# Last attention layer: softmax sink sums and gated splits moved to GpSimd, output panels 0 and 1 split and partly multiplied between the units

## The reference

```
m    = max(sink, max_j s_j)
den  = exp(sink - m) + sum_j exp(s_j - m)
p_j  = exp(s_j - m) / den
o    = sum_j p_j v_j
x   += g * ((o * silu(z)) @ w_out)        # w_out: 1024 x 1024
```

## Time and profile before

| | us |
|---|---|
| median of 3 runs | 1967.74 (1966.52 to 1968.47) |
| the profiled execution, whole | 1967.9 |
| its span, first to last instruction | 1965.7 |
| PE busy | 1928.1 (98% of the span) |
| DVE busy | 1303.1 (66%) |
| ACT busy | 905.4 (46%) |
| GpSimd busy | 52.1 (3%) |

### The profile page before, as it was taken

The page is one execution under the profiler, slowest core; times in us unless marked ns, Lnnn a source line. Parts: engine busy times, 40 slices in busy tenths (PEclk is TensorE's granted clock), DMA queues, the critical chain, the costliest instruction groups (busy, mean ns, idle before and its releaser), DMA issues. The chain is left out here.

```text
span 1965.7 us, 31270 instructions
## 1 busy us (share of the span) xinstructions
PE 1928.1 (98%) x12652; PEld 1619.4 (82%) x12652; DVE 1303.1 (66%) x2407; ACT 905.4 (46%) x1635; POOL 52.1 (3%) x78
## 2 busy tenths in 40 slices
PE   7999999999999999999999999999999999999998
PEld 5788668889888888898689899998887788888867
DVE  5547777857886665667666777675566464555886
ACT  4446863325423232355764655443443432234685
POOL 0000000001000000000000000000000000001000
PEclk9999999999999999999999999999999999999999
DMA  7322016543545455443139455554311133432411
GB/s 314 118 84 99 18 50 234 179 159 108 193 174 208 178 192 190 169 148 108 54 134 338 172 191 195 178 184 161 119 54 54 65 119 118 149 128 86 150 44 44
DMA packets 53583, 278.39 MB, mean 142 GB/s; under 512 B 4536, under 2 KB 19128, under 8 KB 24512
## 3 DMA queue, kind: packets, MB, share of 16 engines
q1 hardware_dynamic: 47168, 265.50, 37.8%
q10 hardware_dynamic: 6128, 10.03, 1.7%
q0 software_dynamic: 144, 0.85, 0.1%
HBM read 274.26 MB, written 2.11 MB: 141 GB/s over the span
## 5 line engine op out<-in xcount | busy, mean ns | idle before, releaser
L640 PE MATMUL ps<-t 128*128 128x512 f32 (+1 forms) x1936 | 665.3, 344 | 2.4 <-DVE t L2035 2.4
L642 PE MATMUL ps<-t 128*128 128x512 f32 (+1 forms) x1936 | 658.8, 340 | 0.0
L641 PE MATMUL ps<-t 128*128 128x512 f32 (+1 forms) x1936 | 658.6, 340 | 0.0
L2035 DVE TENSOR_TENSOR t<-t 128x1024 fp32r<-128x1024 f32 (+2 forms) x370 | 414.1, 1160 | 153.5 <-ACT t L1386 152.6
L1386 ACT ACTIVATE t<-t 128x1024 fp32r<-128x1024 f32 (+3 forms) x376 | 358.3, 1001 | 194.6 <-PE ps L642 142.4
L640 PEld LDWEIGHTS ps<-t 128*128 128x128 f32 x1936 | 363.6, 188 | 52.7 <-DVE t L2035 4.7
L642 PEld LDWEIGHTS ps<-t 128*128 128x128 f32 x1936 | 363.6, 188 | 42.5
L641 PEld LDWEIGHTS ps<-t 128*128 128x128 f32 x1936 | 363.7, 188 | 41.7 <-issue 0.7
L2021 DVE TENSOR_TENSOR t<-t 128x256 f32<-128x256 f32 (+9 forms) x622 | 227.9, 386 | 135.0 <-ACT t L1770 31.2
L2030 DVE SCALAR_TENSOR_TENSOR t<-t 128x256 f32<-128x256 f32 (+4 forms) x372 | 272.8, 765 | 34.1 <-ACT t L1491 21.9
L1491 ACT ACTIVATE t<-ps 128x512 f32<-128x512 f32 (+2 forms) x239 | 113.1, 494 | 289.4 <-PE ps L642 186.9
(11 more groups left out here) (191 smaller groups left out, 2280.5 us busy)
## 6 DMA issues: line engine op xcount, KB each, us to landing
t<-in_panels SPq DMA_DIRECT2D x231, 1024.0 KB, 4.9
t<-in_panels SPq DMA_DIRECT2D x12, 768.0 KB, 4.3
t<-in_panels SPq DMA_DIRECT2D x16, 512.0 KB, 3.6
t<-in_window ACTq DMA_DIRECT2D x4, 768.0 KB, 4.4
t<-gates_between ACTq DMA_DIRECT2D x4, 512.0 KB, 4.9
t<-in_panels SPq DMA_DIRECT2D x1, 1088.0 KB, 5.1
t<-in_ctxT SPq DMA_DIRECT2D x1, 1024.0 KB, 6.6
t<-in_xT SPq DMA_DIRECT2D x1, 1024.0 KB, 8.9
```

Source lines behind the costliest of these rows:

```text
L640: e.matmul(o, hi[:, k, w], xh[:, c0:c1], start=k == 0, stop=False)
L641: e.matmul(o, hi[:, k, w], xl[:, c0:c1], start=False, stop=False)
L642: t = e.matmul(o, lo[:, k, w], xh[:, c0:c1], start=False, stop=k == p.nk - 1)
L2035: e.tensor_tensor(p.half(p.split(wlo), a), p.half(raw[p.slot], a), p.half(p.split(whi), a).bitcast(F32), ALU.subtract).then_inc(*up(ve, (" ...
```

## The change

Four things are edited, all in the last attention.

1. The two sums with the sink (sink - m, and the sink's exponential added to the row sum) leave DVE and go to GpSimd (`sink_units`). DVE's reciprocal now waits for GpSimd's `den`; ACT's sink exponential waits for GpSimd's `sink`.
2. The hi and lo parts of the gated chunks 0 to 6 leave ACT and DVE and go to GpSimd as well (a copy and a subtraction of 128x256). Chunk 7 stays on ACT and DVE.
3. The halves of panels 0 and 1 are split in iterations 4, 6, 8, 10 (ACT) and 5, 7, 9, 11 (DVE) instead of 16 and 17.
4. PE multiplies panel 0's chunks 0 to 5 in iterations 16, 17 and 18, before that iteration's transposes; after the units come chunk 6 of panel 0, chunks 0 to 6 of panel 1, and then chunk 7 of both.

```diff
--- before.py
+++ after.py
@@ -1339,13 +1339,15 @@
                         t = e.transpose(o[:, tile * 128:tile * 128 + 128], aqtok[:, tile, c * 128:c * 128 + 128], ident)
                     t.then_inc(*up(pe, ("full", ("aqT", c))))
 
-                softmax("A", at_units(), aPT, lambda i: gate(3, (4, 5)) if i == 1 else None)
-                for a in range(4):
+                def out_products(a, ks):
                     p = at["atw", a]
-                    weights(p)
+                    if 0 in ks:
+                        for j in range(2):
+                            bank(("atw", 2 * a + j), (2 * a + j,)) if a < 2 else bank(("atw", 2 * a + j))
+                        weights(p)
+                    o = [banks(("atw", 2 * a + j))[:, 0:LAT] for j in range(2)]
                     hi, lo = p.view(p.split(whi)), p.view(p.split(wlo))
-                    o = [bank(("atw", 2 * a + j))[:, 0:LAT] for j in range(2)]
-                    for k in range(8):
+                    for k in ks:
                         rest(p, k)
                         if a == 0:
                             e.wait_ge(*done(("aylo", k)))
@@ -1356,7 +1358,23 @@
                             t = e.matmul(o[j], lo[:, k, w], aYh[:, k, :], start=False, stop=k == 7)
                             if k == 7:
                                 t.then_inc(*up(pe, ("full", ("atw", 2 * a + j))))
-                    used(p)
+                    if 7 in ks:
+                        used(p)
+
+                def among(i):
+                    if i == 1:
+                        gate(3, (4, 5))
+                    if i >= 16:
+                        out_products(0, ((0, 1, 2), (3, 4), (5,))[i - 16])
+
+                softmax("A", at_units(), aPT, among)
+                out_products(0, (6,))
+                out_products(1, range(7))
+                out_products(0, (7,))
+                out_products(1, (7,))
+                banks.next(4)
+                for a in range(2, 4):
+                    out_products(a, range(8))
 
             e.wait_ge(*done("ones"))
             first_sums("c")
@@ -1524,8 +1542,6 @@
                         if u["yh"] is not None:
                             e.wait_ge(*done(("full", ("o", s, i3))))
                             e.activation(u["yh"], banks(("o", s, i3))[:, 0:128 * u["xs"]], ACT.Copy).then_inc(*up(se, ("oh", s, i3)))
-                        elif i3 % 2 == 0 and i3 >= 2:
-                            gate_hi(i3 // 2 - 1)
                     beside(i)
 
             def gate_hi(c):
@@ -1959,8 +1975,10 @@
                 def among_units(i):
                     if i == 1:
                         gate(3)
-                    if i in (16, 17):
-                        hi_to(at["atw", i - 16].i)
+                    if i in (4, 6, 8, 10):
+                        p = at["atw", i // 8]
+                        hi(p, (i // 2 % 2,))
+                        nxt[0] = max(nxt[0], p.i + 1)
 
                 softmax("A", at_units(), aPT, ast, among_units)
                 gate_hi(7)
@@ -2226,15 +2244,10 @@
                         if u["sink"] is not None:
                             own()
                             tt(m, m, u["nsink"], ALU.min, ("max", s, i))
-                            own()
-                            tt(st[2][:, spot[i]], m, u["sink"], ALU.add, ("sink", s, i))
                     if 1 <= i <= n_u:
                         u, par = units[i - 1], (i - 1) % 2
                         r = rs[:, spot[i - 1]]
-                        e.wait_ge(*done(("exp", s, i - 1)))
-                        if u["sink"] is not None:
-                            tt(r, r, st[2][:, spot[i - 1]], ALU.add)
-                            own()
+                        e.wait_ge(*done(("den" if u["sink"] is not None else "exp", s, i - 1)))
                         e.reciprocal(r, r).then_inc(*up(ve))
                         own()
                         w = 512 // u["xs"]
@@ -2253,8 +2266,6 @@
                         u, key = units[i3], ("o", s, i3)
                         e.wait_ge(*done(("full", key)))
                         tt(u["az"], banks(key)[:, 0:128 * u["xs"]], u["az"], ALU.mult, ("read", key), ("az", i3 // 2))
-                        if i3 % 2 and i3 >= 3:
-                            gate_lo(i3 // 2 - 1)
                     beside(i)
 
             def gate_lo(c):
@@ -2708,8 +2719,10 @@
                 def among_units(i):
                     if i == 1:
                         gate(3)
-                    if i in (16, 17):
-                        lo_to(at["atw", i - 16].i)
+                    if i in (5, 7, 9, 11):
+                        p = at["atw", (i - 1) // 8]
+                        lo(p, (i - 1) // 2 % 2)
+                        nxt[0] = max(nxt[0], p.i + 1)
 
                 softmax("A", at_units(), ast, among_units)
                 gate_lo(7)
@@ -2783,6 +2796,26 @@
                         e.tensor_tensor(XAl[:, k, a:b], work[:, k % 4, a:b], XAh[:, k, a:b].bitcast(F32), ALU.subtract).then_inc(
                             *up(po, ("xlo", s, k, x)))
 
+            def sink_units():
+                units = at_units()
+                spot = spots(units)
+                for i in range(len(units) + 3):
+                    if i < len(units):
+                        e.wait_ge(*done(("max", "A", i)))
+                        e.tensor_tensor(ast[2][:, spot[i]], ast[0][:, spot[i]], units[i]["sink"], ALU.add).then_inc(
+                            *up(po, ("sink", "A", i)))
+                    if 1 <= i <= len(units):
+                        r = ast[1][:, spot[i - 1]]
+                        e.wait_ge(*done(("exp", "A", i - 1)))
+                        e.tensor_tensor(r, r, ast[2][:, spot[i - 1]], ALU.add).then_inc(*up(po, ("den", "A", i - 1)))
+                    if i % 2 == 0 and i >= 4 and i < 18:
+                        c = i // 2 - 2
+                        e.wait_ge(*done(("az", c)))
+                        e.tensor_copy(aYh[:, c, :], sz[:, c, :]).then_inc(*up(po))
+                        e.wait_ge(po.sem, po.n)
+                        e.tensor_tensor(aYl[:, c, :], sz[:, c, :], aYh[:, c, :].bitcast(F32), ALU.subtract).then_inc(
+                            *up(po, ("aylo", c)))
+
             e.memset(pick[:, :, :], 0.0).then_inc(*up(po))
             e.wait_ge(po.sem, po.n)
             for x in range(2):
@@ -2802,6 +2835,7 @@
                 rsqrt(ssc, ssc, ("h mean", i), ("h root", i))
             lo(at["atkv", 0])
             norm_mod("s1", "cl")
+            sink_units()
 
 
         for signal in (pe, ve, se, po):
```

## The result

| | before | changed |
|---|---|---|
| median, us (8 runs of each, side by side) | 1968.11 (1966.52 to 1971.02) | 1973.17 (1971.37 to 1975.25) |
| profiled execution, its span | 1967.9, 1965.7 | 1971.37, 1969.6 |

The changed kernel takes 1.0025 times as long as before (95% interval 1.0016 to 1.0034): 5 us more, where 1972.6 was forecast. The median is right; three terms of the sum are not (the way into SBUF, the tail and the clock behind panel 2's wait), and they largely cancel.

The account below looks back on a forecast made before the run. DVE's queue was taken to bound the units, PE the stretch behind them. +6.4 us to unit 15's maximum less 1.5 after it gave +4.9, a median of 1972.6; range 1968.4 to 1979, the forecast's own 1970.3 to 1975.5.

Parts of the forecast that it names:

- Small operations and gated chunks off DVE: In the units, two of DVE's four small operations go, -3.6 us in eleven iterations; gated chunks leaving five iterations, -1.65.
- The round trip: Each iteration DVE waits before its reciprocal for GpSimd's two sums and hand-overs: 0.50 us, +5.5 in eleven iterations.
- Half panels: Four halves on DVE in odd iterations of the units, no longer hidden: 1.18 us each, +4.7.
- The shared way into SBUF: GpSimd's chunk copy and subtraction overlap DVE's small operations and slow them in odd iterations 5 to 13: +1.25 us.
- Iteration 3: This iteration has the round trip without a gated chunk: +0.17 us.
- To the maximum of unit 15: Sum of all terms in the units up to DVE's maximum of unit 15: +6.4 us.
- From there: From unit 15's maximum to the last product, PE packs its waits but waits for panel 2: gain 1.5 us, not 3.3.
- PE keeps its clock: PE stays at its high clock level amid the units, through the hand-over and before panel 2, so no time is added.
- rival (4): PE idles in odd iterations or before panel 2 and falls to the low clock: some 1.7 us, 1974.3; chance 0.06.
- Rival (1): Cheap round trip: GpSimd's two sums overlap (0.3 us) and nothing meets on the way into SBUF: 1969.2; chance 0.22.
- Rival (2): Not slower: `den` is ready when DVE's minimum ends, PE sets the pace at 3.02 us: -0.4 or -2.3; chance 0.09.
- Rival (3): Dear sums on GpSimd: 0.56 us each, a round trip of 1.2, +7.7 more: 1980.3; chance 0.09.

Follow-up runs that it names:

- the second profile: Profile of the changed kernel run once more, unaltered, beside one with panel 2's wait filled: median 1974.71, 1.0025 of before; last maximum to last residual 32.69 us.

## Why the prediction was right, point by point

- **DVE is the bound in the units**: right. All terms of the units fell on the end in full, and taking them back gave them back.
- **Small operations and gated chunks off DVE, -3.6 and -1.65**: right; the first together with the round trip, +0.16 net per iteration by two experiments, the second 1.72.
- **The round trip, 0.50**: 0.46. The hand-overs are 0.09 (1903.14 + 0.35 to 1903.58) and 0.03 (1903.92 to 1903.95), as at 1412 us; the sums are 0.19, and the second starts 0.04 before the first has ended.
- **Half panels, 1.18 each**: 1.12.
- **The shared way into SBUF, +1.25**: this step failed. I gave the copy 0.5 between ends of 0.23 and 0.81; it took 0.40, and the subtraction 0.73. So the pair ended 1.36 after the start of the next maximum (1905.15 to 1906.51), from where I had counted 1.5, and met the small operations for 0.1 at their start. By my own rule (0.3 beyond GpSimd's end, against 1.58) 0.08 would still have been lost; they kept their 0.36, so as a term it is 0.
- **Iteration 3, +0.17**: 0.16 in iterations 2 and 3 together, all of it in iteration 2 (3.08 for 2.91; iteration 3 keeps its 3.29).
- **To the maximum of unit 15, +6.4**: +4.7, and the missing 1.7 is the port term's 1.25, the halves' 0.06 each, and what the sums and iteration 3 came out lower.
- **From there, -1.5**: this step was mis-sized. PE's waits are packed and the wait for panel 2 is 1.86 (1.85 forecast), but even with its clock kept PE ends 1.25 late. It comes to the first products 1.70 after the maximum, not 1.4 (1936.34 - 1934.64): the last maximum had no gated chunk ahead of it any more, so it came earlier against PE. At each change between output products and the transposes or values of a unit PE loses 0.1 (1936.34 to 1936.56 is 0.22 and 1938.42 to 1938.63 is 0.21, against 0.117), which for three groups of output products, each with a change at both ends, is 0.6; and the remaining 0.35 is in the last 60 products and the edges of the wait. These are read from rows, not tried. The Trainium skill says in "TensorEngine Tiling (Array Packing)", section "Key Properties", that a change of tiling mode drains the engine; the 0.1 agrees with that.
- **PE keeps its clock**: right in the units and in the hand-over. Wrong at panel 2's wait in some executions (two of the seven profiles with that wait): that is rival (4), which I gave 0.06, with 1.7 for its price. It measured 1.4 in the second profile. I had argued that dense work ahead of a wait speaks against it; the second profile shows dense work, 1.86 idle, and the lower level.

Put together from the rows: 4.9 forecast, -1.7 in the units, +1.25 in the tail, makes +4.5 for an execution that keeps its clock, and +5.9 for one that loses 1.4 behind panel 2's wait. One more term was held at nothing: outside the span the runs of the changed kernel take 1.8 or 1.9 us, those of before 2.1 to 2.3, some 0.4 less, for a reason that no run shows; that makes +4.1 and +5.5. The median of +5.06 lies between. So the mechanism of the units was right, but that 4.9 came so near is luck: it was met by offsets. The range's upper end is also not the sum of its terms: 1972.6 + 1.1 + 1.25 is 1974.95, not 1975.5. **Rival (1)** had its second half right (no meeting at SBUF) and its first wrong: 0.46, not 0.3. **Rival (2)** named the right switch, the order in GpSimd's queue: turned round, the kernel equals the one before, though DVE and not PE still sets its pace. **Rival (3)** is out: 0.19 per sum, not 0.56.

## What to carry to other kernels

Work that goes to an idle engine costs its round trip wherever that engine's queue holds the result needed next behind something that must still wait; look at the order of its waits first, for here it decided about 4.9 us, more than the work itself (3.6). Don't hold each iteration to another engine's round: 2.71 stood under PE's 2.95 behind an iteration of 3.88, in which PE had got ahead. When products are spread to fill waits, look for the buffer that is freed later by it, and price the wait with what the clock takes behind it.

## What the runs showed of the hardware

- PE idle for up to 1.4 us in every second iteration of the units (8.13 of 10 busy) left the granted clock at 1.00; one idle stretch of 1.86 behind dense products took it to 0.50 for some 3 us in one profile of the changed kernel and not in the other, and in two of seven profiles with that wait in all.
- Two 128x2 sums on GpSimd start 0.15 apart although each is shown as 0.19.
- A GpSimd instruction of 0.19 took 1.25 beside a DVE half panel that had started 0.02 before it, while DVE's own instruction kept its 1.22; a DVE operation of 0.16 that started 0.1 before a GpSimd subtraction ended was not lengthened.
